# Branch b of the prompt attention: 192 keys per half tile of 64 queries without a mask, instead of 256 keys per tile of 128 queries with one

## The reference, cut to what matters

```python
def _sink_attend(q, k, v, valid, sinks):
    s = jnp.einsum('bnqkgd,bnlkd->bnkgql', q, k, preferred_element_type=F32)
    s = jnp.where(valid[None, :, None, None, None, :], s, -jnp.inf)
    ...
    p = jnp.exp(s - m)
    p = p / (p.sum(-1, keepdims=True) + jnp.exp(sk - m))
    return jnp.einsum('bnkgql,bnlkd->bnqkgd', p.astype(v.dtype), v)
```

## Time and profile before

| what | value |
|---|---|
| median of three runs | 3636.93 us (3632.38 to 3639.15) |
| profiled execution, its own time | 3634.75 us |
| its span, first to last instruction | 3633.1 us |
| TensorE matmuls busy | 3259.5 us (90%) |
| TensorE weight loads busy | 2656.5 us (73%) |
| VectorE, ScalarE, GpSimd busy | 1466.5, 896.6, 172.6 us |
| DMA busy, mean of 16 engines | 0.34 of the span |
| prompt attention, branch b, layer 1 | some 909 to 1122 us |
| prompt attention, branch b, layer 2 | some 2691 to 2905 us |

### The profile page before, as it was taken

One profiled execution on the slowest core, in us unless ns is written; L12 is line 12 of the kernel. 1 busy time (PEld: TensorE's weight loads), 2 busy tenths in 40 slices (PEclk: granted clock), 3 DMA queues, 4 the chain that ended last, 5 costly groups with the idle time before them and its releaser, 6 DMA issues. The chain is left out here.

```text
span 3633.1 us, 52418 instructions
## 1 busy us (share of the span) xinstructions
PE 3259.5 (90%) x20718; PEld 2656.5 (73%) x20718; DVE 1466.5 (40%) x3367; ACT 896.6 (25%) x2006; POOL 172.6 (5%) x118
## 2 busy tenths in 40 slices
PE   0999986999999997988969999779999999977988
PEld 0788886777777775667858888767787777745867
DVE  5214234444444442354631143444434444423556
ACT  0221212333223332220121212223332233322110
POOL 0000000100110100000000000010111110000000
PEclk9999998999999998989979999889999999987999
DMA  5322216322333216764342222352223232096633
GB/s 197 110 87 94 84 54 201 86 69 59 88 93 88 83 39 173 228 234 151 127 157 89 91 96 68 115 158 68 69 72 91 85 94 66 30 262 205 217 136 110
DMA packets 405163, 419.73 MB, mean 116 GB/s; under 512 B 154561, under 2 KB 314177, under 8 KB 402561
## 3 DMA queue, kind: packets, MB, share of 16 engines
q1 hardware_dynamic: 371088, 376.87, 33.5%
q10 hardware_dynamic: 33840, 39.66, 3.3%
HBM read 291.17 MB, written 127.64 MB: 115 GB/s over the span
## 5 line engine op out<-in xcount | busy, mean ns | idle before, releaser
L351 PE MATMUL proj_acc<-proj_wh,keep_xh 128*128 128x512 f32 (+1 forms) x1296 | 501.7, 387 | 12.5 <-DVE proj_wl L326 12.5
L1066 PE MATMUL att_gacc<-att_gwh,keep_xh 128*128 128x256 f32 x1728 | 504.6, 292 | 2.5 <-POOL att_gwl L986 2.5
L352 PE MATMUL proj_acc<-proj_wl,keep_xh 128*128 128x512 f32 (+1 forms) x1296 | 500.4, 386 | 0.0
L353 PE MATMUL proj_acc<-proj_wh,keep_xl 128*128 128x512 f32 (+1 forms) x1296 | 500.2, 386 | 0.0
L1068 PE MATMUL att_gacc<-att_gwh,keep_xl 128*128 128x256 f32 x1728 | 486.8, 282 | 0.0
L1067 PE MATMUL att_gacc<-att_gwl,keep_xh 128*128 128x256 f32 x1728 | 485.9, 281 | 0.0
L1150 DVE COPY att_pt<-att_tr 128x256 f32<-128x256 f32 (+3 forms) x384 | 177.2, 461 | 620.9 <-PE att_tr L1031 620.6
L1093 ACT ACTIVATE att_p<-att_ss,att_stat 128x257 f32<-128x257 f32 (+9 forms) x384 | 249.4, 650 | 691.5 <-DVE att_stat L1143 691.5
L1020 PE MATMUL att_ss<-att_kt,att_qt 64*128 64x256 f32 (+9 forms) x1024 | 376.2, 469 | 1.3 <-DVE att_kt L1078 1.3
L1066 PEld LDWEIGHTS att_gacc<-att_gwh,keep_xh 128*128 128x128 f32 x1728 | 326.5, 189 | 17.2 <-issue 10.6
L1067 PEld LDWEIGHTS att_gacc<-att_gwl,keep_xh 128*128 128x128 f32 x1728 | 326.2, 189 | 0.0
(11 more groups left out here) (294 smaller groups left out, 4393.5 us busy)
## 6 DMA issues: line engine op xcount, KB each, us to landing
scratch_gates<-att_gout SPq DMA_DIRECT2D x216, 128.0 KB, 1.7
up_gates<-scratch_gates SPq DMA_DIRECT2D x18, 1536.0 KB, 8.0
proj_raw<-in_w_in SPq DMA_DIRECT2D x48, 512.0 KB, 3.7
att_graw<-in_w_in SPq DMA_DIRECT2D x48, 512.0 KB, 3.7
str_ka<-in_cache_a_kT SPq DMA_DIRECT2D x16, 1024.0 KB, 9.7
str_va<-in_cache_a_v SPq DMA_DIRECT2D x16, 1024.0 KB, 5.4
scratch_sg<-proj_out SPq DMA_DIRECT2D x54, 256.0 KB, 2.0
att_sg<-scratch_sg SPq DMA_DIRECT2D x24, 512.0 KB, 6.0
```

The source lines that it names most:

```text
L351: nc.tensor.matmul(bank, hi, wh[:, u, kt, 0:w], start=kt == 0, stop=False)
L352: nc.tensor.matmul(bank, hi, wl[:, u, kt, 0:w], start=False, stop=False)
L353: mm = nc.tensor.matmul(bank, lo, wh[:, u, kt, 0:w], start=False, stop=kt == KT - 1)
L1066: nc.tensor.matmul(gacc[:, 0:GW], hi, gwh[:, n % 2, k, :], start=k == 0, stop=False)
```

## The change

For tiles 1 to 7 of branch b (`dense`) the score is made by two matmuls, one per half of 64 queries, each over its own 192 keys and on its own 64 columns of the array, and nothing is added for a mask. The maximum and the exponential run over 192 keys and the sink. The second of a sub's two transposes has 64 columns. The values are made by halves: for each half 128 keys and then 64 keys, for both heads; the second half, whose keys start 64 later, takes v from a copy that is shifted by 64 tokens and loaded beside the first by two more DMAs (columns 64 to 127 of v's tiles, free in branch b). Tile 0 and the branches a and c stay as they are.

```diff
+def dense(kind, a):
+    return kind == "b" and a > 0
+
+def width(kind, a):
+    return P + HD if dense(kind, a) else len(window(kind, a)) * P
...
+    def vs_count(n):
+        return sum(64 if UNITS[i][0] == "b" else 32 for i in range(n % 2, n + 1, 2))
...
                     sp.dma_start(v[:, n % 2, :, 0:HD], src).then_inc(vs_loaded[n % 2], 16)
+                    cols = slice(pair // 2 * HD, pair // 2 * HD + HD)
+                    shifted = S["vb"][HD:SEQ - HD].rearrange("(t p) c -> p t c", p=P)[:, :, cols]
+                    sp.dma_start(v[:, n % 2, 0:PT - 1, HD:P], shifted).then_inc(vs_loaded[n % 2], 16)
+                    sp.dma_start(v[0:HD, n % 2, PT - 1, HD:P], S["vb"][SEQ - HD:SEQ, cols]).then_inc(vs_loaded[n % 2], 16)
...
-                first, w = window(kind, a)[0] * P, len(window(kind, a)) * P
+                first, w = window(kind, a)[0] * P, width(kind, a)
+                if dense(kind, a):
+                    for half in range(2):
+                        at = half * HD
+                        mm = nc.tensor.matmul(ss[at:at + HD, s, 0:w], qt[0:HD, n % 2, u, a * P + at:a * P + at + HD],
+                                              keys(kt, n, u)[:, first + at:first + at + w], start=True, stop=True,
+                                              skip_group_check=True, tile_position=(0, at))
+                    mm.then_inc(s_made, 1)
+                    return
...
-                        mm = nc.tensor.transpose(tr[:, g % 2, (j % 4) * P:(j % 4 + 1) * P], p[:, m % 2, j * P:(j + 1) * P],
-                                                 C["ident"][:])
+                        w = min(P, width(kind, m // 2) - j * P)
+                        mm = nc.tensor.transpose(tr[0:w, g % 2, (j % 4) * P:(j % 4 + 1) * P],
+                                                 p[:, m % 2, j * P:j * P + w], C["ident"][:])
...
+            def dense_value(n, a):
+                for half in range(2):
+                    cols = slice(half * HD, half * HD + HD)
+                    for j, t, w in ((0, a - 1, P), (1, a, HD)):
+                        for u in range(2):
+                            at = j * P + half * HD
+                            mm = nc.tensor.matmul(oo[u * HD:u * HD + HD, cols], v[0:w, n % 2, t, cols],
+                                                  pt[0:w, u, at:at + HD], start=j == 0, stop=j == 1,
+                                                  skip_group_check=True, tile_position=(0, u * HD))
+                mm.then_inc(pv_made, 1)
...
-                    pe.wait_ge(vs_loaded[n % 2], 32 * (n // 2 + 1))
+                    pe.wait_ge(vs_loaded[n % 2], vs_count(n))
...
+                if dense(kind, a):
+                    dense_value(n, a)
+                    return
...
-                w = len(window(kind, m // 2)) * P + (kind == "b")
+                w = width(kind, m // 2) + (kind == "b")
...
-                w = len(window(kind, m // 2)) * P
+                w = width(kind, m // 2)
...
-                        dve.wait_ge(vs_loaded[n % 2], 32 * (n // 2 + 1))
+                        dve.wait_ge(vs_loaded[n % 2], vs_count(n))
```

## The result

The changed kernel takes 3645.41 us in the median of 18 runs (3637.64 to 3655.73), the kernel before 3637.32 us in 18 (3631.98 to 3649.23). The ratio is 1.0025 with an interval from 1.0015 to 1.0035: 5 to 13 us slower, where no difference was forecast. The time is inside the range that was forecast, 3626 to 3648 us, but it lies clear of no change. The profiled execution took 3649.8 us.

The account below looks back on a forecast made before the run. TensorE's stream bounds branch b's units, GpSimd's chain their ends. Eight units at 0 and two passages from a to b at -0.63 make -1.3 us: median 3635.6 us, no difference, range 3626 to 3648.

Parts of the forecast that it names:

- Price of a group of 64 columns, values: Branch b's values: four groups at 0.26 us make 1.04 us instead of 0.59, 0.45 more per value.
- rival without a drain between 128x64 and 64x64: Inside a value: the two modes follow freely, a value stays at 0.59 us, kernel 3617.7 us; chance 0.07.
- Scores by halves at once: Branch b's scores: both halves run together; score to gate takes 0.54 us instead of 0.75; 11 scores save 2.24 us.
- rival of halves one after the other: Branch b's scores: halves run in sequence, 384 steps, 0.33 us more per score, kernel about 3671 us; chance 0.05.
- Loads inside a group exposed: Value groups and scores: each head's second load stands open, 0.05 us each, +13 us, 3650 us; chance 0.03.
- Inside a unit nothing: Branch b, fill 0 to fill 8: scores -2.24 us and five values +2.25 us cancel.
- From a to b -0.63: Passage from branch a to b: no dense value, shorter scores save 0.63 us, twice, -1.3 us.
- Added loads at nothing: SyncE's queue: two added loads, 0.38 us each to issue, cost nothing, their data being needed some 50 us later.
- From b to c 0: Passage from branch b to c: two values' 0.90 us more hide in 1.31 us of TensorE idle, cost 0.
- At the ends of units between b and b 0, hidden behind GpSimd: Fill 8 to next fill 0: TensorE reaches the gate 0.27 us later, within 0.43 to 0.65 us of waiting, cost 0.
- The base of the sum: Whole kernel: profiled execution of 3634.75 us, 2.2 us under the median of 3636.93, from which the terms were counted.

Follow-up runs that it names:

- e1: Changed kernel with each value's groups ordered by height, both 128-key groups first, then both of 64 keys: 3635.9 us, ratio 0.9996 to the kernel before.
- e2: Changed kernel with only its scores by halves, values as before the change: 3633.2 us, ratio 0.9983 to the kernel before.
- e5: Changed kernel without its two added loads of shifted v, the wait again counting 32: 3647.7 us, ratio 1.0024 to the kernel before.
- e13: Changed kernel with half the next unit's fill weights loaded after fill 6's store, and fill 8 in slot 14 instead of 13: 3625.1 us, ratio 0.9968.
- e8: Kernel before with q and k of branch b given a 65th row, as in branch a: 3616.5 us, ratio 0.9928.
- e14: Kernel before with half the next unit's fill weights loaded after fill 6's store, and fill 8 in slot 14 instead of 13: 3616.6 us, ratio 0.9946.
- e12: Changed kernel with values ordered by height, one start flag per head and the earlier load of fill weights: 3626.3 us, ratio 0.9962 to the kernel before.

## Why the forecast was wrong, step by step

- **Price of a group of 64 columns, values:** right. Forecast 1.04 us, measured 1.06. The rival without a drain between 128x64 and 64x64 is out. The Trainium skill's rule that a change of tiling mode drains the engine ("TensorEngine Tiling (Array Packing)", Tiling Modes) holds here for 128x64 against 64x64: ordering the groups by height took 0.30 us off a value, 1.06 to 0.76 (e1).
- **Scores by halves at once:** right, 0.53 against 0.54. The rival of halves one after the other is out. The 11 scores of a unit save 2.02 us (e2), forecast 2.24.
- **Loads inside a group exposed:** out, since that rival needs 1.24 us for a value and 1.06 was measured. The rule of the Trainium skill ("TensorE: Matmul & The Clock Gate", Part 3, The mechanism), that a load overlaps only where its row group differs, isn't what these traces show: the fills' loads, 0.19 us each and all in the same 128 rows, overlap with matmuls that start every 0.12 us.
- **Inside a unit nothing:** nearly right, 0.24 us per unit where no fall precedes (unit 4). **From a to b -0.63:** measured -0.65 from the last fill of unit 3 to the first of unit 4.
- **Added loads at nothing:** right (e5).
- **From b to c 0:** wrong, though small. The end of unit 7 takes 9.03 and 8.98 us instead of 8.59 and 8.53, without a fall. The sum set 0.90 us of values against 1.31 us that the first fill of unit 8 waited. But the later values push VectorE's product for the gate (L1160 before, L1201 after) back beside GpSimd's split: it takes 2.28 us instead of 0.59, and the gate waits for it.
- **At the ends of units between b and b 0, hidden behind GpSimd:** this step failed, and it is the one that the result hangs on. I asked when TensorE would come to the gate, 0.27 us later against 0.43 of slack, and took the clock of 1.00 as given, although the forecast counted it among the things to look at. The end of a unit is the longest stretch of branch b without a fill, 8.75 us; the change spreads two values over 0.9 us more for the same columns and takes columns out of three scores. The clock falls to 0.50 there, and the slack and more is used up: 8.75 becomes 9.4 to 10.0, and 1.3 to 2.1 us more follow in the next unit. That these ends are where the clock falls, and that a fill put into them stops half of the falls (e13), is shown; what exactly in the stretch brings the clock down isn't.
- **The base of the sum.** The profile of before showed 1.00 throughout branch b, and the scatter of three runs was narrow. It was one side of an edge: another execution of the same kernel has five falls there, and the average one has some 10 us more at 0.50, over the whole program, than that profile.

## What to carry to other kernels

Where a stretch has no dense matmuls, a change that leaves the critical path alone can still lower TensorE's clock, as it did here, and most of the price is then paid in the dense work behind the stretch. One profile with a clock of 1.00 doesn't show how close the kernel is to falling; the clocks of all runs say more. Before splitting matmuls, count the changes of tile height: each cost 0.15 us here in a value (0.30 for two, e1) and 0.1 around a score (0.20 for two, e8); order the work by height, or pad the odd operand by a row. Look for the long thin stretches in the order of work and put a dense piece into them: moving one of nine fills by one slot, with an earlier load, was worth 17 us to the kernel before (e14), twice what the change cost.

## What was not expected of the hardware

- The granted clock fell to 0.50 with TensorE's records busy for 4.02 of the 4.54 us before and a single gap of 0.52 us. The kernel before is busy for the same 4.02 us there and keeps 1.00, so the busy share of the records didn't tell which of the two would fall.
- The same program has falls in one execution and not in the next, 3635 and 3658 us.
- A start flag on columns 64 to 127 of a bank, set between two matmuls of a group in columns 0 to 63, makes the second one of that group write instead of add; e12 sets it once per head. This is inferred from the outputs of e1 and e12, which differ in this and the earlier load; no trace shows it.
